# A transformer block on one Trainium2 core: one of seven FFN-in block products replaced by seven quarter-size products

## What is computed

```python
def swiglu(h, w_in_ffn, w_out_ffn):
    g, u = jnp.split(h @ w_in_ffn, 2, axis=-1)
    return (jax.nn.silu(g) * u) @ w_out_ffn

xl = xl + gt2 * swiglu(modulate(rms_norm(xl, g_ffn[l]), sh2, sc2), w_ffn_in[l], w_ffn_out[l])
return rms_norm(xl, g_final)
```

## Time and profile before

| what | value |
|---|---|
| runs of the kernel before | 1262.05, 1262.78, 1264.39 us (median 1262.78) |
| the profiled execution | 1262.73 us, of which span 1260.9 us |
| PE busy | 1236.5 us (98%) |
| DVE, ACT, POOL busy | 912.0, 651.5, 344.9 us |
| granted PE clock | 0.998 of full speed |
| steady pair of FFN-in | 36.27 us |

### The profile page before, as it was taken

The page is one execution under the profiler, slowest core; times in us unless marked ns, Lnnn a source line. Parts: engine busy times, 40 slices in busy tenths (PEclk is TensorE's granted clock), DMA queues, the critical chain, the costliest instruction groups (busy, mean ns, idle before and its releaser), DMA issues.

```text
span 1260.9 us, 22752 instructions
## 1 busy us (share of the span) xinstructions
PE 1236.5 (98%) x7872; PEld 650.3 (52%) x7872; DVE 912.0 (72%) x1517; ACT 651.5 (52%) x1238; POOL 344.9 (27%) x341
## 2 busy tenths in 40 slices
PE   8999999999999999999999999999999999999997
PEld 1564656556665666664454444444444444444443
DVE  3879998666779999954368866676666665667586
ACT  2532234556779999963145655444444543412324
POOL 0100000114678999840013322233332210000001
PEclk9999999999999999999999999999999999999999
DMA  9728723235200130021130332222223305997953
GB/s 354 275 75 325 255 81 134 68 93 158 64 25 2 34 133 16 18 84 51 50 100 1 93 92 83 78 68 70 75 83 91 91 28 159 358 341 253 365 181 134
DMA packets 108165, 158.91 MB, mean 126 GB/s; under 512 B 8384, under 2 KB 67264, under 8 KB 106816
## 3 DMA queue, kind: packets, MB, share of 16 engines
q1 hardware_dynamic: 108096, 158.00, 36.8%
HBM read 135.95 MB, written 19.93 MB: 124 GB/s over the span
## 4 chain that ended last, share of the span: by engine, by line
PE 71%; DVE 10%; ACT 9%; issue 6%; POOL 2%; DMA 1%; ACTq 0%; SPq 0%; POOLq 0%; DVEq 0%
PE PS L1222 67%; ACT arena L2129 4%; DVE arena L2553 1%; PE PS L1550 1%; PE PS L1487 1%; PE PS L1296 1%; ACT PS L2132 1%; ACT arena L2132 1%; DMA arena<-weight_sum_rows 1%; DVE arena L3187 1%; DMA arena<-in_w_mod 1%; DVE arena L3190 1%; DVE arena L3067 1%; DVE arena L2949 1%; POOL arena L1093 1%
## 5 line engine op out<-in xcount | busy, mean ns | idle before, releaser
L1222 PE MATMUL PS<-arena 128*128 128x512 f16 (+8 forms) x7272 | 1195.1, 325 | 15.6 <-DMA arena<-in_w_mod 4.8
L1222 PEld LDWEIGHTS PS<-arena 128*128 128x128 f16 (+3 forms) x7272 | 599.4, 100 | 584.6 <-issue 43.7
L2949 DVE SCALAR_TENSOR_TENSOR arena<-arena 128x512 f16<-128x512 f32 x148 | 120.7, 822 | 76.6 <-ACT arena L2217 76.6
L2217 ACT ACTIVATE arena<-arena 128x512 f16<-128x512 f32 x140 | 87.6, 629 | 130.4 <-PE PS L1222 130.4
L2841 DVE TENSOR_REDUCE arena<-PS 128x1 f32<-128x512 f32 (+1 forms) x160 | 106.6, 682 | 8.9 <-PE PS L1222 8.9
L2329 ACT ACTIVATE arena<-arena 128x512 f16<-128x512 f32 x77 | 48.1, 629 | 121.9 <-DVE arena L3100 73.5
L2129 ACT ACTIVATE arena<-PS 128x512 f16<-128x512 f32 x140 | 88.2, 630 | 1.2 <-PE PS L1222 0.7
L1189 POOL TENSOR_TENSOR arena<-arena 128x512 f32<-128x512 f32 x20 | 26.7, 1336 | 222.0 <-DMA arena<-in_w_ffn_in 193.8
L1093 POOL TENSOR_TENSOR arena<-arena 128x512 f16<-128x512 f32 x64 | 73.9, 1156 | 9.4 <-ACT arena L2132 8.1
L1216 POOL TENSOR_TENSOR arena<-arena 128x1 f32<-128x1 f32 x8 | 4.7, 597 | 236.1 <-DVE arena L3241 236.1
L2865 DVE TENSOR_TENSOR arena<-PS,arena 128x512 f16<-128x512 f32 x96 | 65.5, 682 | 4.0 <-ACT PS L2132 3.9
(11 more groups left out here) (208 smaller groups left out, 1168.1 us busy)
## 6 DMA issues: line engine op xcount, KB each, us to landing
arena<-in_w_ffn_out SPq DMA_DIRECT2D x121, 256.0 KB, 4.8
arena<-in_w_mod SPq DMA_DIRECT2D x23, 1024.0 KB, 7.3
arena<-in_w_ffn_in SPq DMA_DIRECT2D x88, 256.0 KB, 3.0
arena<-in_w_in SPq DMA_DIRECT2D x9, 1024.0 KB, 5.5
left_operands<-arena SPq DMA_DIRECT2D x33, 256.0 KB, 2.2
arena<-left_operands SPq DMA_DIRECT2D x3, 2816.0 KB, 12.4
arena<-lay_bias SPq DMA_DIRECT2D x12, 512.0 KB, 3.8
arena<-in_x SPq DMA_DIRECT2D x2, 2048.0 KB, 14.3
```

The source lines that it names most:

```text
L1222: return pe.matmul(out, lhsT, rhs, start=start, stop=stop, skip_group_check=True)
L2217: act.activation(aS[n % RING][:, 0], weight_block(p, b), ACT.Copy, scale=WS).then_inc(blk_hi, 1)
L2949: dve.scalar_tensor_tensor(dst[:, 1], src, WS, dst[:, 0], ALU.mult, ALU.subtract).then_inc(blk_lo, 1)
```

## The change

P2 of pairs 1 to 10 is no longer one product per hidden block. Its operand A12 over both hidden blocks (512 features x 256 columns) is cut into 2 x 2 blocks again, and so are the 512 x 512 token data, and the same scheme of seven products is used a second time: m1 to m7, each of 2 k-tiles x 3 half combinations = 6 matmuls of 128 x 128 weights on 256 tokens. Four groups G of them (three, two, one and one products) stand between the other steps. The sums of token data (T2) are made once, on DVE and ACT, ahead of pair 1. Four sums of weight blocks of 256 columns (`second_sums`) are made on POOL per pair. ACT and DVE split 1792 columns of P2's weights per pair in three pieces ("a" 512, "b" 256, "s" 1024) where it was 1024 in two. m1, m6, m7 and m4 run into one PSUM bank, one on top of the other, with a read by DVE between them; m2, m5 and m3 into another. DVE makes six additions (`second_add`: five of 256 columns, one of 512) where it made two of 512. RING is 6, the ring holds the 12 other blocks only. The left operand S3 is the fourth that goes to DRAM, and comes back in FFN-out by one more `load_left`. P1 is copied out earlier, P5 and the silu of the gate later. The diff, cut to its core:

```diff
-STEPS = [(p, b) for p in ("P2", "P1", "P5", "P6", "P7", "P3", "P4") for b in range(2)]
+STEPS = [("G", 0), ("P1", 0), ("P1", 1), ("P5", 0), ("P5", 1), ("G", 1), ("P6", 0), ("G", 2), ("P6", 1), ("G", 3),
+         ("P7", 0), ("P7", 1), ("P3", 0), ("P3", 1), ("P4", 0), ("P4", 1)]
+WHOLE = [s for s in STEPS if s[0] != "G"]
+BLOCKS = [("P1", 0), ("P2", "a"), ("P1", 1), ("P2", "b"), ("P5", 0), ("P2", "s")] + WHOLE[3:]
-RING = 7
+RING = 6
+ADDS = ("m1", "m5", "u2", "c0", "u3", "c1", "up0", "up1", "g0", "g1")
+SECOND_STEPS = (("m1", "m2", "m5"), ("m6", "m3"), ("m7",), ("m4",))
+SECOND_AT = {"m1": (3, 0), "m6": (3, 0), "m7": (3, 0), "m4": (3, 0), "m2": (1, 0), "m5": (1, 256), "m3": (1, 256)}
-KEPT_OUT = ("A22", "S1", "S4")
+KEPT_OUT = ("A22", "S1", "S4", "S3")
...
-                keep_left(it, ("A22", "S1"))
+                keep_left(it, ("A22", "S3", "S1"))
...
             load_fo(3 * KQ, 3 * KQ + 4)
+            load_left(KEPT_OUT.index("S3"))
             sp.wait_ge(fo_mm, 4 * (DOWN.index("P2") + 1))
...
+            def second_sums(pair, first=False):
...
+                for b in range(2):
+                    pool.wait_ge(fi_in["A12", b], pair * 16 + 16)
...
+                pool.tensor_tensor(s1, a10, a11, ALU.add).then_inc(s_rdy, 1)
+                pool.tensor_tensor(s3, a00, a10, ALU.subtract).then_inc(s_rdy, 1)
+                pool.wait_ge(s_rdy, at + 1)
+                pool.tensor_tensor(s2, s1, a00, ALU.subtract).then_inc(s_rdy, 1)
+                pool.wait_ge(s_rdy, at + 3)
+                pool.tensor_tensor(s4, a01, s2, ALU.subtract).then_inc(s_rdy, 1)
...
+            def second(g, pair, first=False):
+                if g == 0:
+                    pe.wait_ge(blk_lo, blocks_before(pair) + block_no("P2", "s") + 1)
...
+                else:
+                    pe.wait_ge(fi_sum, added(pair, (None, "m5", "u2", "u3")[g]))
+                for m in SECOND_STEPS[g]:
+                    w, right = SECOND[m]
+                    bank, o = SECOND_AT[m]
+                    for k in range(2):
+                        for part, other in ((0, 0), (0, 1), (1, 0)):
...
+                            ins = mm(PS[:, bank, o:o + 256], W2[:, part, 2 * w + k, :], src,
...
+            def next_hi(j, pair, last=False):
+                w, pair = j + RING, pair
+                if w < len(WHOLE):
+                    block_hi(*WHOLE[w], pair)
+                elif not last:
+                    block_hi(*WHOLE[w - len(WHOLE)], pair + 1)
+                    if w - len(WHOLE) < 3:
+                        block_hi("P2", "abs"[w - len(WHOLE)], pair + 1)
...
+                elif name == "u3":
+                    done(pair, "G", 2)
+                    dve.wait_ge(fi_sum, added(pair, "m5"))
+                    add(gated1[1][:, right], PS[:, 3, left])
...
+                for n, (p, b) in enumerate(STEPS):
+                    if (p, b) == ("P6", 0):
+                        second_add("u2", pair)
+                        second_add("c0", pair)
+                    if (p, b) == ("P6", 1):
+                        second_add("u3", pair)
+                    if (p, b) == ("P7", 0):
+                        second_add("c1", pair)
...
+                    if p != "G":
+                        next_lo(WHOLE.index((p, b)), pair, last)
...
+                    if (p, b) == ("P1", 1):
+                        second_add("m1", pair)
...
+                    if (p, b) == ("P5", 0):
+                        second_add("m5", pair)
                         operand_lo("S1", pair - 1)
...
+                    if (p, b) == ("P6", 0):
+                        operand_lo("S2", pair - 1)
+                    if (p, b) == ("G", 2):
+                        operand_lo("S4", pair - 1)
```

More of the change, by code:

```diff
@@ L132, in steps_before, with blocks_before, block_no, added @@
     return (pair - 1) * NSTEP + NPLAIN
+def blocks_before(pair):
+    return (pair - 1) * NBLOCK + NPLAIN
+def block_no(p, b):
+    return BLOCKS.index((p, b))
+def added(pair, name):
+    return (pair - 1) * NADD + ADDS.index(name) + 1
+def snapped(pair, p, b):
+    return (pair - 1) * len(SNAPS) + SNAPS.index((p, b)) + 1
 def chunk_index(kind, n):
@@ L496, in build @@
         F11, F21 = f32(20, 4, 512), f32(28, 4, 512)
-        F12, F22, Tf = f32(Z + 60, 4, 512), f32(Z + 68, 4, 512), f32(Z + 76, 4, 512)
+        F12, F22, Tf = f32(Z + 8, 4, 512), f32(Z + 24, 4, 512), f32(Z + 16, 4, 512)
+        T2 = f16(Z + 66, 4, 2, 2 * 256)
+        T2f = [f32(Z + 74 + 2 * i, 2 * 256) for i in range(4)]
+        W2 = f16(Z + 74, 2, 14, P)
+        W2f = f32(Z + 84, 8, P)
         Ts = {p: f16(o, 4, 2, 512) for p, o in (("P5", 20), ("P6", 36), ("P7", 44), ("P4", 28))}
@@ L513, in build @@
                                                    ("S1", 52), ("A22", 74), ("S4", Z))}
-        staged = [hT[:, :, i, 512:1024] for i in range(3)]
+        staged = [hT[:, :, i, 512:1024] for i in range(4)]
         first_half = [f32(Z + 91, 512), f32(Z + 93, 512)]
@@ L990, in _ @@
             load_fo(FO_RAW, KQ)
-            keep_left(NPAIR - 1, KEPT_OUT)
+            keep_left(NPAIR - 1, ("A22", "S3", "S1", "S4"))
             def load_x2(n):
@@ L1210, in _ @@
             with pool.Fori(0, NPAIR - 2) as it:
+                second_sums(it + 2)
                 for p in SUMS:
@@ L1807, in operand @@
             def operand(p, part, k):
-                if p in ("P1", "P2"):
-                    return hT[:, part, k + (4 if p == "P2" else 0), 0:512]
+                if p == "P1":
+                    return hT[:, part, k, 0:512]
                 if p == "P3":
@@ L2254, in silu @@
             def silu(which, b, pair):
-                act.wait_ge(fi_sum, (pair - 1) * 6 + 4 * which + b + 1)
+                act.wait_ge(fi_sum, added(pair, f"{'cg'[which]}{b}"))
                 buf = (gated1, gated2)[which][b]
@@ L2287, in _ @@
             plain_silu(0, 0)
+            for i in range(4):
+                act.wait_ge(t_f, i + 1)
+                act.copy(T2[:, i, 0], T2f[i]).then_inc(t_hi, 1)
             for i in range(8):
@@ L2295, in token_sum_hi @@
                 for i in range(4):
-                    n = 4 * list(Ts).index(p) + i
+                    n = 4 + 4 * list(Ts).index(p) + i
                     act.wait_ge(t_f, n + 1)
@@ L2304, in _ @@
             plain_silu(1, 0)
-            for n in range(4):
-                block_hi(n, 1, True)
+            for p, b in BLOCKS[:6]:
+                block_hi(p, b, 1, True)
             act.wait_ge(x1_out[2], 32)
@@ L2310, in _ @@
             token_sum_hi("P4")
-            for n in range(4, 7):
-                block_hi(n, 1, True)
+            for p, b in BLOCKS[6:RING + 3]:
+                block_hi(p, b, 1, True)
             def right_hi(q):
@@ L3080, in _ @@
             plain_gated(1, 0)
-            for n in range(4):
-                block_lo(n, 1)
+            for p, b in BLOCKS[:6]:
+                block_lo(p, b, 1)
             token_sum("P7")
@@ L3126, in pair_steps @@
             def pair_steps(pair, first=False, last=False):
-                for n in range(NSTEP):
-                    if n in (8, 9):
-                        up_sum(n - 8, pair)
-                    if n in (10, 11):
-                        gate_sum(1, n - 10, pair)
-                    if n == 11:
-                        gated(1, 0, pair)
-                    if n in (12, 13):
-                        gated(0, n - 12, pair)
-                    if not last or n + RING < NSTEP:
-                        block_lo(n + RING, pair)
-                    if n == 0:
+                for n, (p, b) in enumerate(STEPS):
+                    if (p, b) == ("P6", 0):
[5 more added lines that the diff above has]
+                        second_add("c1", pair)
+                    if p == "P7":
+                        up_sum(b, pair)
+                    if p == "P3":
+                        gate_sum(b, pair)
+                    if (p, b) == ("P3", 1):
+                        gated(1, 0, pair)
+                    if p == "P4":
+                        gated(0, b, pair)
+                    if p != "G":
+                        next_lo(WHOLE.index((p, b)), pair, last)
+                    if (p, b) == ("G", 0):
```

262 lines of the change are left out of this document (173 added, 89 removed).

## The result

The changed kernel takes 1282.41 us (median of 6 runs, 1280.29 to 1285.18), the kernel before 1262.97 beside it (1261.24 to 1264.39). The ratio is 1.0151, 95% interval 1.014 to 1.0163: slower by 19.4 us by the medians, 19.1 by the ratio. The forecast was 1278 us, in a range of 1265 to 1286. The profiled execution of the changed kernel took 1281.33 us.

The account below looks back on a forecast made before the run. The prediction took PE, busy 98%, to bound the kernel. From 1262.7 us it summed -6.0 (PE), +17.2 (G3's waits), +4.1 (pair 1) and +0.4 (FFN-out) to 1278.4, forecast 1278 us, range 1265 to 1286.

Parts of the forecast that it names:

- PE saves 6.0: P2's products on PE: 42 small matmuls of 0.109 us replace 24 of 0.216, -6.0 us over ten pairs.
- upper bound of 0.116: Time per 256-column matmul on PE with the drain counted; only 0.31 us a pair would be saved.
- fourth rival: Small matmuls on PE: weight loads don't hide behind 109 ns, 2.9 us less saved, 1281 us; chance 5%.
- G3 waits on u3: Last group: PE waits for DVE's addition, late in its list and slowed by POOL; 1.85 us in nine pairs, +17.2 in all.
- E: The end of a PE step from which waits are counted; here the end of P6 block 0.
- first rival: Ahead of G3, POOL's sums miss the chain of u3; every pair waits only 0.59 us, 1266.7 us; chance 14%.
- Pair 1, +4.1: Ahead of G1 in the first pair, DVE is behind with m5: PE waits 4.5 us, less 0.37 from before.
- step on turn taking: In pair 1, DVE takes turns with POOL's sums; without any, DVE would reach m5 about 4 us earlier.
- FFN-out, +0.4: S3's returning load delays P5's weight blocks by 7.7 us; cover just used up, 0 to 1 us, taken as +0.4.
- third rival: From P7 to P4, DVE falls behind as POOL slows its low halves: up to 0.8 us a pair, 1285; chance 7%.

Follow-up runs that it names:

- the version without waits: P4's token sums left out (part of the computation missing), on top of the changed kernel with u3 first and S3's load later: 1256.60 us, ratio 0.9954 to the kernel before.

## Why the prediction was right, and where it was not

- **PE saves 6.0.** Right: 0.1095 us a small matmul (0.109 taken), and 6.0 us over the FFN once no wait is in the way (582.79 against 589.28, less 0.5 for the old wait). The upper bound of 0.116 falls, with the fourth rival. By the spacing of 131 and 81 ns that the Trainium skill gives ("TensorE: Matmul & The Clock Gate", section "Back-to-back issue gap") and the prediction weighed, the version without waits would be slower than before on PE; it is 6 us faster.
- **G3 waits on u3.** Right in place, mechanism and size. DVE's low half at E + 1.49 (1.48 forecast), u3's start at E + 4.69 (4.41 to 4.78), PE at E + 5.16 (4.94 to 5.31), the wait 1.90 (1.85). Undoing the order took all of it away, undoing POOL's part left 0.47 (0.59). Summed over the pairs, 15.2 us shown and 1.6 of drains, 16.8 against 17.2. Two errors partly cancel in that: the loop's waits came out 0.05 us longer than counted, and the two ends shorter (1.26 lost in pair 1 against 1.85, 0.38 in pair 10 against 0.59). The first rival (POOL misses the chain) falls: its sums started at E + 1.23, 0.4 later than forecast (from the low half that releases A12's load to POOL's start it took 3.52 us, not 3.12), but still ahead of all three operations.
- **Pair 1, +4.1.** The size is right (4.11 shown, 4.27 lost, less 0.37), but by luck: the step on turn taking failed. I had DVE's sums lengthened by POOL ahead of `gated`, as in the earlier trace rows, and `gated` at 699.25. In the trace DVE was not slowed at all up to `gated`, POOL was:

```profile
681.17 15.57 POOL L1245 TENSOR_TENSOR arena<-arena 128x512 f32<-128x512 f32 x2 [10.92 <-DVE arena L3069]
684.23 2.49 DVE L3214 TENSOR_TENSOR arena<-arena 128x512 f32<-128x512 f32 x4
...
693.87 0.68 DVE L3174 SCALAR_TENSOR_TENSOR arena<-PS,arena 128x512 f32<-128x512 f32 x1
694.47 1.16 DVE L3069 SCALAR_TENSOR_TENSOR arena<-arena 128x512 f16<-128x512 f32 x1
695.11 0.63 ACT L2321 ACTIVATE arena<-arena 128x512 f16<-128x512 f32 x1 [2.39 <-POOL arena L1245]
695.77 3.20 DVE L3069 SCALAR_TENSOR_TENSOR arena<-arena 128x512 f16<-128x512 f32 x2 [0.15 <-ACT arena L2321]
...
698.90 1.75 DVE L3189 TENSOR_TENSOR arena<-arena 128x512 f32<-128x512 f32 x1
...
705.72 0.41 DVE L3119 TENSOR_TENSOR arena<-PS,arena 128x256 f32<-128x256 f32 x1
```

DVE works at its own 0.60 us a step and is at `gated` at 693.87, about 4 us sooner than forecast (this execution's FFN starts 1.3 us sooner). POOL gets through only there: its first sum ends at 695.08, and the next three run to 700.10. In that time four operations of DVE take 6.1 us instead of 2.4 (694.47 to 700.57). Of the 3.7 us lost 0.3 are two waits of 0.15 for ACT's high halves, which had waited for POOL; the rest are operations lengthened to 1.16, 1.52, 1.53 and 1.75. So the collision that I had charged ahead of `gated` came behind it, at nearly the same price (about 4), and the wait was back at 4.1.
- **What came behind that wait** is missing from the sum. The 42 matmuls behind it (24 of 512 columns, 18 of 256) took 9.00 us; the same number of each took 7.32 at the full clock, behind a wait of 1.54 us, in the version with the groups further back and u2 first. That is 1.7 us.
- **FFN-out, +0.4.** This term was mis-sized: it is 3.15 us shown and 3.5 lost with two drains. The first wait is the one that I had counted, with a cover too small. The fourth block's low half stands in DVE's list behind the sum of the fifth, and the fifth comes behind S3. DVE waited 13.70 us for it:

```profile
1163.05 0.69 DVE L3274 TENSOR_TENSOR arena<-arena 128x512 f32<-128x512 f32 x1 [13.70 <-DMA arena<-in_w_ffn_out]
```

S3's load took 18.0 us from issue to landing (its row in the queue, and the time to landing of this one load):

```profile
1138.17 0.87 SPq L1045 DMA_DIRECT2D arena<-left_operands  x1
...
DMA to landing us min/median/max: 18.0/18.0/18.0
```

Most of that is its place in the queue. The loads of this stretch land one after the other: the last block ahead of S3 at 1147.97, S3 at 1156.19. So S3 itself held the queue for 8.2 us, near the 7.7 that I had by bandwidth. What I had taken as unchanged is the rest: the block ahead of S3 landed 8.03 us ahead of P5's start in the kernel before (1131.44, 1139.47) and 6.67 in the changed one (1147.97, 1154.64). So the fifth block came 8.2 + 1.4 = 9.6 us later against PE, 1.9 over the cover, and PE lost 2.0. Why the loads ahead had slipped stays open. The second wait is missing from my count: S4's load was issued 18.0 us ahead of P3's start before and 11.5 here, took as long (12.4 and 12.8), and landed 1.3 us late. With S3 behind the rest of P5's blocks both waits went.
- **From P7 to P4** the low halves did get longer, two in 3.41 us at 795.43, as the third rival had it, but no wait came of it, not even with PE 1.9 us further ahead.
- **The sum.** FFN: -6.0 + 16.8 + 3.9 + 1.7 + 3.5 = 19.9, measured 19.9. Forecast 15.7. The 4 us between them are the clock (1.7) and FFN-out (3.5 against 0.4), less 0.6 in the other terms.

## What to carry to other kernels

When a large product is cut into small ones that wait for additions, the gain on the bound engine is small and sure (6 us here) and the loss hangs on where the other engine's list has the additions. Count from the end of the step that releases them, and put each addition directly behind its release, ahead of work that nobody waits for: that alone was worth 16.8 us. If the list is full there, as in pair 1, moving its work about gives nothing back; let the bound engine do one step more between a group and the addition it needs. A cover that the count finds "just used up" has no room for a slip of the transfers ahead: 1.4 us of it and 0.5 of the new transfer's own time came out as 2.0 us of waiting here. Count the transfers behind the new one too: S4's load, issued 64 us after S3's, came 1.3 us late until S3 was moved.
